# Turning the FFN hidden blocks on TensorE instead of on VectorE and the DMA queues

## The reference

```python
def swiglu(x, w13, w2):
    gate, up = jnp.split(x @ w13, 2, axis=-1)
    return (jax.nn.silu(gate) * up) @ w2

h = h + 0.5 * rms_norm(swiglu(rms_norm(h, g[0]), ffn_w13[i, 0], ffn_w2[i, 0]), g[1])
```

## Time and profile before

| | |
|---|---|
| median of three runs | 2231.45 us |
| profiled execution | 2231.45 us |
| its span, first to last instruction | 2229.6 us |
| mean granted TensorE clock | 0.997 of full speed |
| TensorE busy | 2193.2 us (98%) |
| VectorE, ScalarE, GpSimd busy | 68%, 51%, 42% |
| HBM read | 392.37 MB, 176 GB/s over the span |

### The profile page before, as it was taken

One profiled execution on the slowest core, in us unless ns is written; L12 is line 12 of the kernel. 1 busy time (PEld: TensorE's weight loads), 2 busy tenths in 40 slices (PEclk: granted clock), 3 DMA queues, 4 the chain that ended last, 5 costly groups with the idle time before them and its releaser, 6 DMA issues.

```text
span 2229.6 us, 34582 instructions
## 1 busy us (share of the span) xinstructions
PE 2193.2 (98%) x13031; PEld 1785.4 (80%) x13031; DVE 1519.0 (68%) x2167; ACT 1148.0 (51%) x1668; POOL 943.2 (42%) x1694
## 2 busy tenths in 40 slices
PE   8999999999999999999999999999999999999998
PEld 6888888888888758878887888878888788868886
DVE  6766757766775877686667766656766776677665
ACT  5545545545554454255455455465545554565544
POOL 4761005751673110438714761004861575056741
PEclk9999999999999999999999999999999999999999
DMA  8766656764776640067656765535765676526752
GB/s 268 214 218 203 226 174 208 219 207 170 234 215 210 199 158 12 5 217 219 224 181 206 213 225 193 181 96 163 221 212 197 197 219 213 188 72 219 217 198 104
DMA packets 335155, 418.81 MB, mean 188 GB/s; under 512 B 34280, under 2 KB 238384, under 8 KB 334992
## 3 DMA queue, kind: packets, MB, share of 16 engines
q1 hardware_dynamic: 285072, 377.20, 52.3%
q0 software_dynamic: 49776, 39.36, 5.9%
q10 hardware_dynamic: 144, 0.07, 0.0%
HBM read 392.37 MB, written 1.05 MB: 176 GB/s over the span
## 4 chain that ended last, share of the span: by engine, by line
PE 94%; DVE 3%; ACT 1%; issue 1%; POOL 1%; DMA 0%; DVEq 0%; POOLq 0%; SPq 0%; ACTq 0%
PE bank L522 29%; PE bank L523 28%; PE bank L524 28%; PE bank L536 1%; PE bank L2563 0%; PE bank L1452 0%; PE bank L2557 0%; ACT JUNK L631 0%; PE bank L2574 0%; PE bank L1967 0%; ACT wh L624 0%; PE bank L2534 0%; PE bank L1189 0%; DVE H L875 0%; DVE qPS L1905 0%
## 5 line engine op out<-in xcount | busy, mean ns | idle before, releaser
L808 DVE TENSOR_TENSOR wl<-raw,wh 128x1024 fp32r<-128x1024 f32 x708 | 857.2, 1222 | 517.7 <-ACT wh L624 512.1
L624 ACT ACTIVATE wh<-raw 128x1024 fp32r<-128x1024 f32 x708 | 744.3, 1058 | 727.5 <-PE bank L524 703.4
L1080 POOL DMA_DIRECT2D AF<-att x1408 | 762.2, 550 | 167.2 <-DVE att L932 144.2
L522 PE MATMUL bank<-wh,XH 128*128 128x512 f32 x2000 | 792.8, 396 | 6.5 <-DVE wl L808 5.3
L523 PE MATMUL bank<-wl,XH 128*128 128x512 f32 x2000 | 780.2, 390 | 0.0
L524 PE MATMUL bank<-wh,XL 128*128 128x512 f32 x2000 | 780.1, 390 | 0.0
L522 PEld LDWEIGHTS bank<-wh,XH 128*128 128x128 f32 x2000 | 376.2, 188 | 98.2 <-issue 18.5
L524 PEld LDWEIGHTS bank<-wh,XL 128*128 128x128 f32 x2000 | 376.2, 188 | 79.6
L523 PEld LDWEIGHTS bank<-wl,XH 128*128 128x128 f32 x2000 | 376.6, 188 | 74.6 <-issue 0.5
L522 PE MATMUL bank<-wh,AH 128*128 128x512 f32 x704 | 275.2, 391 | 0.0
L524 PE MATMUL bank<-wh,AL 128*128 128x512 f32 x704 | 274.0, 389 | 0.0
(11 more groups left out here) (339 smaller groups left out, 1801.4 us busy)
## 6 DMA issues: line engine op xcount, KB each, us to landing
raw<-in_ffn_w_dram SPq DMA_DIRECT2D x182, 512.0 KB, 4.8
raw<-in_ffn_wi_dram SPq DMA_DIRECT2D x176, 512.0 KB, 4.8
raw<-in_ffn_w_dram SPq DMA_DIRECT2D x40, 1024.0 KB, 5.3
raw<-in_ffn_wo_dram SPq DMA_DIRECT2D x40, 1024.0 KB, 5.2
AF<-att POOLq DMA_DIRECT2D x1408, 16.0 KB, 3.8
raw<-in_a_wqkv_dram SPq DMA_DIRECT2D x18, 1024.0 KB, 5.0
raw<-in_a_w_in_dram SPq DMA_DIRECT2D x16, 1024.0 KB, 5.2
raw<-in_b_w_in_dram SPq DMA_DIRECT2D x12, 1024.0 KB, 5.0
```

The source lines that it names most:

```text
L522: pe.e.matmul(o, a, h, start=(k == 0), stop=False)
L624: act.e.activation(self.wh[j % N_W][:, 0:p.size], self.raw[p.chunk % N_RAW][:, p.at:p.at + p.size], ACT.Copy).then_inc(*self.rounded.up(j))
L808: dve.e.tensor_tensor(self.wl[j % N_W][:, 0:p.size], self.raw[p.chunk % N_RAW][:, p.at:p.at + p.size], self.wh[j % N_W][:, 0:p.size].bitca ...
L1080: pool.e.dma_start(whole[32 * j:32 * j + 32, :, i, :], hid[32 * i:32 * i + 32, :, j, :]).then_inc(*self.d_hid[b % 3].up(n, b, i, j, by=16))
```

## The change

The hidden blocks are turned on TensorE. A new helper `pe_turn_hidden` issues four transposes of 128x128 (two halves of the block by two token tiles) into one of the two turning banks. It is called in "up" at step 32 (block 0) and at steps 44, 60, ... 172 (blocks 1 to 9), and in "out" at step 12 (block 10). `act_hidden` and `dve_hidden` read that bank instead of `AF`, and move: block 0 ahead of the `round`/`leave` of part 7 of "up", block b ahead of that of part 4b+6, block 10 at part 2 of "out". VectorE's transpose of squares, GpSimd's 16 DMAs for each block, the buffer `AF` and their semaphores go. The hidden block in `att` is laid out plainly, token tile by token tile.

```diff
+    def pe_turn_hidden(self, pe, n, b):
+        bank = self.turn_bank(pe, ("hid", n, b), (self.hid_hi, n, b), (self.hid_lo, n, b))
+        hid = self.att[b % 3]
+        for i in range(2):
+            for t in range(T):
+                pe.wait_ge(self.gated, n, b, t)
+                m = pe.e.transpose(bank[:, i * S + t * P:i * S + (t + 1) * P],
+                                   hid[:, t * FB + i * P:t * FB + (i + 1) * P], self.ident[:, :])
+        m.then_inc(*self.turned.up("hid", n, b))
...
+            if step == 32:
+                self.pe_turn_hidden(pe, n, 0)
+            elif step >= 44 and (step - 44) % 16 == 0:
+                self.pe_turn_hidden(pe, n, (step - 44) // 16 + 1)
...
         def down(step):
+            if step == 12:
+                self.pe_turn_hidden(pe, n, NFB - 1)
...
     def act_hidden(self, act, n, b):
-        act.wait_ge(self.d_hid[b % 3], n, b, 3, 3)
-        act.e.activation(self.AH[:, 2 * b:2 * b + 2, :], self.AF[:, 2 * b:2 * b + 2, :], ACT.Copy).then_inc(
+        bank = self.bank(self.place["turn", ("hid", n, b)])
+        act.wait_ge(self.turned, "hid", n, b)
+        act.e.activation(self.AH[:, 2 * b:2 * b + 2, :], bank.rearrange("p (k s) -> p k s", k=2), ACT.Copy).then_inc(
             *self.hid_hi.up(n, b))
...
-            if i >= 12 and i % 4 == 0:
-                self.act_hidden(act, n, i // 4 - 3)
+            if i == 7:
+                self.act_hidden(act, n, 0)
+            elif i >= 10 and i % 4 == 2:
+                self.act_hidden(act, n, i // 4 - 1)
...
-    def dve_turn_squares(self, dve, n, b):
-
-        hid = self.att[b % 3]
-        dve.wait_ge(self.gated, n, b, 1)
-        dve.e.transpose(hid[:, :], hid[:, :]).then_inc(*self.squares_turned.up(n, b))
...
-        for b in range(NFB):
-            self.pool_hidden(pool, n, b)
         self.pool_out(pool, n)
```

More of the change, by code:

```diff
@@ L311, in __init__ @@
         self.AL = at("AL", EO + FF // P * S * 4, [P, FF // P, S], F32R)
-        self.AF = at("AF", EO + FF // P * S * 4, [P, FF // P, S], F32)
         self.CT = [at(f"CT{i}", EO + 54784 + 2048 * i, [P, 4, P], F32) for i in range(2)]
@@ L427, in __init__ @@
         self.hid_hi, self.hid_lo = count("hid_hi"), count("hid_lo")
-        self.squares_turned = count("squares_turned")
-        self.d_hid = [count(f"d_hid{i}") for i in range(3)]
         self.weighed, self.msum, self.rstd, self.resid = (count(x) for x in ("weighed", "msum", "rstd", "resid"))
@@ L452, in bank @@
         return self.banks[i // 2][:, (i % 2) * 512:(i % 2) * 512 + 512]
-    def hidden(self, b, t):
-        return self.att[b % 3][:, :].rearrange("p (k t c) -> p k t c", k=2, t=T)[:, :, t, :]
     def cols(self, n, *key):
@@ L671, in act_out @@
             tail = i - (len(layer.parts) - layer.tail)
-            if STAGES[n][0] == "ffn" and i in (0, 4, 8):
-                self.act_hidden(act, n, NFB - 3 + i // 4)
+            if STAGES[n][0] == "ffn" and i == 2:
+                self.act_hidden(act, n, NFB - 1)
             if i == half - 1:
@@ L749, in act_ffn @@
                     if b >= 3:
-                        act.wait_ge(self.d_hid[b % 3], n, b - 3, 3, 3)
-                    act.e.activation(self.hidden(b, t), self.pair((n, "up", b))[t][:, 0:FB].rearrange(
-                        "p (k c) -> p k c", k=2),
+                        act.wait_ge(self.turned, "hid", n, b - 3)
+                    act.e.activation(self.att[b % 3][:, t * FB:(t + 1) * FB], self.pair((n, "up", b))[t][:, 0:FB],
                                      ACT.Tanh, scale=sc[:, t:t + 1]).then_inc(*self.tanh.up(n, b, t))
@@ L887, in dve_out @@
         for i, p in enumerate(layer.parts):
-            if STAGES[n][0] == "ffn" and i in (0, 4, 8):
-                self.dve_hidden(dve, n, NFB - 3 + i // 4)
+            if STAGES[n][0] == "ffn" and i == 2:
+                self.dve_hidden(dve, n, NFB - 1)
             if i == half - 1:
@@ L923, in dve_hidden @@
     def dve_hidden(self, dve, n, b):
-        hi, lo, whole = (x[:, 2 * b:2 * b + 2, :] for x in (self.AH, self.AL, self.AF))
+        bank = self.bank(self.place["turn", ("hid", n, b)])
+        hi, lo = (x[:, 2 * b:2 * b + 2, :] for x in (self.AH, self.AL))
         dve.wait_ge(self.hid_hi, n, b)
-        dve.e.tensor_tensor(lo, whole, hi.bitcast(F32), ALU.subtract).then_inc(*self.hid_lo.up(n, b))
-    def dve_turn_squares(self, dve, n, b):
-        hid = self.att[b % 3]
-        dve.wait_ge(self.gated, n, b, 1)
-        dve.e.transpose(hid[:, :], hid[:, :]).then_inc(*self.squares_turned.up(n, b))
+        dve.e.tensor_tensor(lo, bank.rearrange("p (k s) -> p k s", k=2), hi.bitcast(F32), ALU.subtract).then_inc(
+            *self.hid_lo.up(n, b))
     def dve_p(self, dve, n):
@@ L946, in dve_ffn @@
                 self.dve_p(dve, n)
-            if i >= 12 and i % 4 == 0:
-                self.dve_hidden(dve, n, i // 4 - 3)
+            if i == 7:
+                self.dve_hidden(dve, n, 0)
+            elif i >= 10 and i % 4 == 2:
+                self.dve_hidden(dve, n, i // 4 - 1)
             self.leave(dve, p.j + N_W)
@@ L952, in dve_ffn @@
                 for t in range(T):
-                    x = self.hidden(b, t)
-                    pair = self.pair((n, "up", b))[t].rearrange("p (s k c) -> p s k c", s=2, k=2)
+                    x = self.att[b % 3][:, t * FB:(t + 1) * FB]
+                    pair = self.pair((n, "up", b))[t]
                     dve.wait_ge(self.tanh, n, b, t)
-                    dve.e.scalar_tensor_tensor(x, x, 1.0, pair[:, 0], ALU.add, ALU.mult).then_inc(
+                    dve.e.scalar_tensor_tensor(x, x, 1.0, pair[:, 0:FB], ALU.add, ALU.mult).then_inc(
                         *self.gate.up(n, b, t))
                     dve.wait_ge(self.gate, n, b, t)
-                    dve.e.scalar_tensor_tensor(x, x, sc[:, T + t:T + t + 1], pair[:, 1], ALU.mult,
+                    dve.e.scalar_tensor_tensor(x, x, sc[:, T + t:T + t + 1], pair[:, FB:2 * FB], ALU.mult,
                                                ALU.mult).then_inc(*self.gated.up(n, b, t))
-                self.dve_turn_squares(dve, n, b)
         self.dve_out(dve, n)
```

## The result

The changed kernel takes 2273.23 us (median of four, 2271.8 to 2273.41) against 2231.45 us for the kernel before (2229.82 to 2232.45): 41.8 us slower, or 1.9%. A second comparison (experiment 12) gave 2273.15 against 2232.6 us, 40.5 us. The forecast was 2275.2 us, range 2269 to 2281.

A forecast was written before the change was run, and what follows sets the result against it. TensorE was taken as the bound, never waiting through the FFN stages. 2231.45 us plus 43.7 us for 88 groups of transposes, with removals at zero and moved work and waits hidden, gave 2275.2 us, range 2269 to 2281.

The forecast's parts named there:

- The bound: Through the FFN stages TensorE never waits, one matmul every 226.7 ns; whatever is put into its stream comes on top.
- the sum: 88 groups of transposes in TensorE's stream at 0.497 us each: 43.7 us, or 40.9 to 44.0 by the bounds.
- The price: Each group of four transposes on TensorE moves the stream by 0.497 us, read from `pe_turn_p` in "up".
- The choice of distance over duration: TensorE's transposes priced by how far four move the stream, 0.497 us, not by the 272 ns each lasts.
- The waits: No group on TensorE waits for its hidden block: 3.21 us to spare for blocks 2 to 10, less for block 0.
- Copies: Operand halves read from PSUM: 0.60 us on ScalarE, 0.68 on VectorE; 2 us less and 2 us more, both hidden.
- What the change removes: GpSimd's 1408 small DMAs (762.2 us) and VectorE's 88 transposes of squares (62.6 us), costed at zero.
- a quicker pace: Rival: matmuls in "up" quicken without the old path, giving back 56.3 us, for 2218.9 us; chance 0.02.
- the no-change case: Rival: the groups fall into TensorE's idle time, or the old path was the cost: 2231 us; chance 0.01.
- lateness at block 0: Rival: block 0 waits 1 us in each stage, 8 us more: 2283 us; chance 0.05, mostly for smaller amounts.
- the unoverlapped price: Rival: the 352 transposes on TensorE don't overlap, 0.272 us each, 95.7 us: 2327 us; chance 0.02.
- the fallen clock: Rival: each group brings a stretch of half clock on TensorE, 123 us more: 2398 us; chance 0.02.

The follow-up runs named there:

- experiment 12: The changed kernel run once more, unaltered, beside the kernel before on the same chip: 2273.15 us against 2232.6 us.
- experiments 7 and 9: 7: the changed kernel with 1408 small DMAs put back on GpSimd's queue, 2273.05 us; 9: the kernel before without VectorE's transposes of squares, 2232.0 us.
- experiment 1: The kernel before with its old path whole, plus 88 groups of four transposes whose result nobody reads: 2276.34 us, ratio 1.018.
- experiments 3 and 5: 3: the changed kernel with eight transposes in each group, 2308.27 us; 5: the changed kernel with 32 in each group, 2537.59 us.
- experiment 4: The changed kernel with the groups of two blocks put together, same number of transposes, 40 interruptions less: 2269.71 us.
- experiment 6: The changed kernel with each group cut in two, two transposes ahead of each of two neighbouring steps: 2273.0 us.

## Why the prediction was right

*The bound.* TensorE was the bound and stayed it: the same waits, the same pace between groups, less idle time, not more. The forecast had read most of the 36.4 us of idle time as lying at the ends of stages; 19.8 us of it lie in the first 25 us of the program and behind its last matmul. Nothing in the sum hung on that, but it hid the one term that was missed. Work taken from VectorE and GpSimd gave nothing back in mid-stage; experiments 7 and 9 put it back or take it away by themselves and move nothing.

*The price.* 0.497 us for each group was read from a helper that already did the same thing at the same kind of step. The groups measured 0.495 in the mean, 88 of them 43.6 us, and experiment 1 shows 44.7 us for them alone (44.0 by the spans). The choice of distance over duration was the one that mattered: by durations the change would have cost 95.7 us.

*The waits.* The forecast had 3.21 us to spare for blocks 2 to 10 and 0.69 us for block 0 of stage 0. After the change the block of the group at 1054.45 is gated at 1050.75 + 0.48 = 1051.23:

```profile
1050.75 0.48 DVE L969 SCALAR_TENSOR_TENSOR att<-att,ST,bank 128x256 f32<-128x256 f32 x1
```

That leaves 3.22 us, 3.21 or 3.22 for all blocks 2 to 10, 1.68 for block 0 and again 0.69 in stage 0. None waited.

*Clock.* 1.00 in every window read behind the start, with a group of four (1020 to 1040 us of the changed kernel), without one (1140 to 1160) and with one of 32. *Copies.* ScalarE's copy takes 0.599 us and VectorE's 0.691 from PSUM, against 0.60 and 0.68 taken from `pe_turn_p`.

*What the sum lacked.* It came out 2 to 3 us high, 43.7 against 41.8 and 40.5. What the change removes, costed at zero, was not quite zero: without the old path's transfers and their three semaphores the program ends 2.9 us sooner. 43.6 - 2.9 = 40.7 us. The profile before had this as a wait of SyncE at the very end, outside what I had read. The time fell inside the range in spite of that only because the term was small: the range was made for other reasons.

The rivals: a quicker pace is excluded by the timeline (226.7 ns between groups), the no-change case by the time, lateness at block 0 by the waits, the unoverlapped price and the fallen clock by experiments 3 and 5.

## What to carry to other kernels

Where one engine runs without a gap, moving work onto it from engines with slack costs its full price, however clumsy the old path looks: 1408 DMAs and 88 transposes of squares were free here but for 2.9 us at the end of the program, and four transposes in their place cost half a microsecond each time. Price an added instruction by how far the same thing already moves the stream in the trace, start to start over some dozens of instructions, not by its duration. If it has to be done, it matters little how it is grouped: pairs of groups gave 3.5 us back (experiment 4), and cutting each group in two cost nothing (experiment 6). And look at the last few microseconds of the program as a stage of its own.

## What was not expected of the hardware

A group of transposes in a stream of matmuls costs 0.147, 0.25, 0.495, 0.89 and 3.51 us for 1, 2, 4, 8 and 32 of them: between 0.11 and 0.15 us for each, where one by itself is recorded with 0.27.

88 times some 3.4 us of nothing but transposes leave the granted clock at 1.00 (0.999 in the mean of the execution). The Trainium skill (TensorE: Matmul & The Clock Gate, Part 4: PE-mode transpose) says that they don't count as TensorE activity in the way matmuls do; in this kernel, with matmuls on both sides, that costs nothing.

The end of the program depends on what GpSimd's DMAs count on: SyncE waits 3.1 us with three further semaphores, 0.5 us with one, and 0.2 us with none.
